# Two more slots in a weight ring of sixteen, a third gather from its own token numbers, and bias products ahead of gathered rows, in a hybrid decoder layer with 32 experts

## The reference

```python
logits = (xt @ w_router + b_router)          # 512 tokens, 32 experts
top_val, top_idx = lax.top_k(logits, 4)
gates = jax.nn.softmax(top_val, axis=-1)
# for each expert e and the rows xb that chose it:
hu = xb @ w1[e] + b1[e]                      # 1024 -> 2048
x_glu, x_lin = min(hu[:, :1024], 7), clip(hu[:, 1024:], -7, 7)
act = x_glu * sigmoid(1.702 * x_glu) * (x_lin + 1)
y = act @ w2[e] + b2[e]                      # 1024 -> 1024
# y times the gate is added to its token, then rmsnorm(x, g_final)
```

## Time and profile before

| | us |
|---|---|
| median of 3 runs | 1233.77 |
| lowest and highest run | 1233.51, 1235.34 |
| the profiled execution's own time | 1230.28 |
| its span | 1228.6 |
| TensorE products busy | 1152.6 (94%) |
| VectorE, ScalarE, GpSimd busy | 306.3, 191.4, 173.3 |
| DMA moved | 454.39 MB, mean 370 GB/s |

### The profile page before, as it was taken

How to read it: one execution, slowest core, us unless ns; L and a number is a source line. 1 busy time by engine, 2 the same in 40 slices (tenths; PEclk the granted TensorE clock), 3 DMA queues, 4 the chain that set the end, 5 groups by cost and what they waited for, 6 DMA issues and landing times. The chain is left out here.

```text
span 1228.6 us, 16404 instructions
## 1 busy us (share of the span) xinstructions
PE 1152.6 (94%) x7022; PEld 477.3 (39%) x7022; DVE 306.3 (25%) x484; ACT 191.4 (16%) x378; POOL 173.3 (14%) x250
## 2 busy tenths in 40 slices
PE   5999997899999999999999999999999999999980
PEld 4777786223333333333333323333333333333330
DVE  5678757321011010101101010110101011010118
ACT  5443522010110100001100000110000011000002
POOL 6000100521101111110111111111111111111000
PEclk9999998899999999999999999999999999999996
DMA  9500675699999999999999999999999999999996
GB/s 336 150 1 20 232 302 193 225 377 403 423 426 426 428 425 426 425 426 427 426 423 427 428 425 426 427 424 427 425 427 426 425 426 426 426 423 428 427 388 242
DMA packets 51147, 454.39 MB, mean 370 GB/s; under 512 B 13044, under 2 KB 13316, under 8 KB 26400
## 3 DMA queue, kind: packets, MB, share of 16 engines
q1 hardware_dynamic: 42864, 434.16, 85.2%
q0 software_dynamic: 7632, 17.05, 3.6%
q10 hardware_dynamic: 576, 2.10, 0.4%
HBM read 442.60 MB, written 15.12 MB: 373 GB/s over the span
## 5 line engine op out<-in xcount | busy, mean ns | idle before, releaser
L849 PE MATMUL ps<-ring_a,blockT 128*64 128x512 f32 x1472 | 325.3, 594 | 8.2 <-DMA ring_a<-in_w 8.1
L1310 DVE TENSOR_SCALAR xnT<-ps 128x768 f32<-128x768 f32 (+1 forms) x32 | 26.9, 841 | 814.7 <-PE ps L856 517.2
L849 PEld LDWEIGHTS ps<-ring_a,blockT 128*64 128x64 f32 x1472 | 101.8, 137 | 217.5 <-issue 195.0
L875 PE MATMUL ps<-ring_a,actT 128*64 128x512 f32 x736 | 165.3, 596 | 1.6 <-DMA ring_a<-in_w 1.6
L849 PE MATMUL ps<-ring_b,blockT 128*64 128x512 f32 x448 | 99.7, 595 | 6.3 <-DMA ring_b<-in_w 6.3
L1597 ACT ACTIVATE blockT<-ps 128x512 f32<-128x512 f32 x30 | 17.9, 597 | 553.0 <-PE ps L796 553.0
L1783 POOL DMA_INDIRECT scores<-h_rows,slots x30 | 31.7, 1056 | 505.7 <-PE ps L796 504.9
L856 PE MATMUL ps<-ring_a,blockT 128*32 128x512 f32 x768 | 91.5, 615 | 0.0
L875 PEld LDWEIGHTS ps<-ring_a,actT 128*64 128x64 f32 x736 | 49.9, 136 | 94.5 <-issue 89.6
L1799 POOL DMA_INDIRECT expert_rows<-normed,slots x32 | 32.6, 1019 | 269.9 <-ACT normed L1626 269.6
L875 PE MATMUL ps<-ring_b,actT 128*64 128x512 f32 x288 | 64.7, 596 | 0.0
(11 more groups left out here) (300 smaller groups left out, 1062.1 us busy)
## 6 DMA issues: line engine op xcount, KB each, us to landing
ring_a<-in_w SPq DMA_DIRECT2D x144, 2048.0 KB, 29.7
ring_b<-in_w SPq DMA_DIRECT2D x48, 2048.0 KB, 31.2
ring<-in_w_in SPq DMA_DIRECT2D x12, 768.0 KB, 18.3
ring<-expert_rows SPq DMA_DIRECT2D x16, 512.0 KB, 14.1
X<-in_x SPq DMA_DIRECT2D x8, 512.0 KB, 6.5
ring<-in_w_out SPq DMA_DIRECT2D x8, 512.0 KB, 4.6
h_rows<-normed ACTq DMA_DIRECT2D x4, 512.0 KB, 3.5
out<-ring SPq DMA_DIRECT2D x4, 512.0 KB, 2.6
```

Of the source, the lines that this page charges most:

```text
L849: ins = mm(ps[half * HALF:(half + 1) * HALF, b, :], x_of(k)[0], ring(r)[:, 0, at + half * 512:at + (half + 1) * 512], start=False, stop=(k ...
L875: ins = mm(ps[half * HALF:(half + 1) * HALF, bank, :], actT[:, s % 2 * W2_K + j, s // 2 * HALF:(s // 2 + 1) * HALF], ring(r)[:, 0, j * D + ...
L1310: v.tensor_scalar(width(glu_c, big), width(ps_glu, big), LIMIT, None, ALU.min).then_inc(glu_ready, 1)
```

## The change

The ring gets eighteen slots. The new two, `ring_c`, lie over `xnT`, and the activation buffers move from there to the memory behind `scores`, over `probsT`; `act_v` becomes the same buffer as `glu_c`. So the first pair of block 0's w2 goes to slots 16 and 17, waits only for the router's logits, and every later pair waits for a release that lies one pair further back. Since `act_v` is now `glu_c`, block 0's activations must be turned before block 1's are clamped: `turn_act_of(0)` moves into the middle of block 1's first product. The third block's token numbers are found as those of the first two (`PICKED = 3`): VectorE picks them ahead of `list_entries`, TensorE sums them in the middle of block 0's first product, and GpSimd gathers them behind its sixteen list writes. The bias products become a function of their own, `w1_bias`, which stands ahead of the wait for rows; for block 0 it stands ahead of the wait for the sort. The returned rows (`y_rows`) lie in slots 6 to 13.

```diff
-RING = 16
+RING = 18
+RING_B = 4
+ROWS_AT = 6
...
 STATIC = 2
+PICKED = 3
...
+        ring_c = sb_r("ring_c", [P, RING - PER - RING_B, SLOT], nc.sbuf_base - KT * SEQ * 4, F32)
...
+        work_at = nc.sbuf_base - HEADS * 2 * P * 4 - HEADS * P * 4
+        glu_c = sb_r("glu_c", [P, PART], work_at, F32)
+        lin_c = sb_r("lin_c", [P, PART], work_at + PART * 4, F32)
+        rowsT = sb_r("rowsT", [P, KT, MANY], work_at + 2 * PART * 4, F32)
+        blockT = sb_r("blockT", [P, 6, P], work_at + 2 * PART * 4, F32)
+        sig = sb_r("sig", [P, PART], work_at + 3 * PART * 4, F32)
+        act_v = glu_c
...
             load_first(12)
-            for k in range(0, W2_SLOTS, 2):
+            sp.wait_ge(logits_done, TB)
+            load_w2(0, 0, w2_slot(0, 0))
+            for k in range(2, W2_SLOTS, 2):
                 wait_free(w2_slot(0, k) + 1)
                 load_w2(0, k, w2_slot(0, k) % RING)
...
             mm(ps[0:E, 4, E:2 * E], ones_bf[:, 0:E], chosen_cum[:, TB, :], start=True, stop=True).then_inc(counts_done, 1)
+            pe.wait_ge(biases_ready, 2)
+            pe.wait_ge(cur_ready, 1)
+            w1_bias(BIG[0], 0)
             pe.wait_ge(sort_ready, 1)
...
+            def third_sums():
+
+                pe.wait_ge(pick_ready, 3 * TB)
+                for t in range(TB):
+                    for part in range(2):
+                        ins = mm(ps[:, 3, 0:1], pick[:, 0, t, :], tok_value[:, t, part:part + 1],
+                                 start=(t == 0 and part == 0), stop=(t == TB - 1 and part == 1))
+                ins.then_inc(tok_summed, 1)
+
             def first_product(i, parity):
 
-                pe.wait_ge(rows_ready, 2 * (i + 1))
-                pe.wait_ge(cur_ready, i + 1)
                 if i:
+                    pe.wait_ge(cur_ready, i + 1)
                     pe.wait_ge(glu_ready, i)
                     pe.wait_ge(lin_ready, i)
+                    w1_bias(BIG[i], parity)
+                pe.wait_ge(rows_ready, 2 * (i + 1))
                 w1_product(BIG[i], parity, lambda k: (w1_slot(i, k) % RING, *arrived[w1_slot(i, k)]),
-                           x_of_lines if i < STATIC else x_of_parts)
+                           x_of_lines if i < PICKED else x_of_parts,
+                           amid=(third_sums, lambda: turn_act_of(0))[i] if i < 2 else None)
...
-                if i == 1:
-                    turn_act_of(0)
...
+            def pick_third():
+
+                chosen_ranks, masked = (picked.rearrange("p t k e -> p (t k e)")[:, n * TB * E:(n + 1) * TB * E].rearrange("p (t e) -> p t e", t=TB) for n in range(2))
+                then(v.scalar_tensor_tensor(out=chosen_ranks, in0=chosen[:, :, :], scalar=-1024.0, in1=ranks[:, :, :], op0=ALU.mult, op1=ALU.add))
+                then(v.scalar_tensor_tensor(out=masked, in0=where[:, 0:E].unsqueeze(1).to_broadcast([P, TB, E]), scalar=float(PICKED - 1),
+                                            in1=chosen_ranks, op0=ALU.is_equal, op1=ALU.mult))
+                then(v.tensor_reduce(own_rank[:, :, 0], masked, AX_X, ALU.add))
+                for t in range(TB):
+                    v.tensor_scalar(pick[:, 0, t, :], iota_r[:, :], own_rank[:, t, 0:1], None, ALU.is_equal).then_inc(pick_ready, 1)
...
+            pick_third()
             list_entries()
+            third_tokens()
...
+            pool.wait_ge(tok_ready, 2)
+            pool.wait_ge(rows_turned, 2)
+            fetch(2)
             pool.wait_ge(list_written, 16 * (1 + TB * TOPK))
```

More of the change, by code:

```diff
@@ L53 @@
 MANY = HALF + QUARTER
+PART = MANY * KT
 HALVES, QUARTERS = range(2)
@@ L240, in layer_kernel, with y_rows @@
         gated_y = normed
-        glu_c, lin_c, sig, act_v = (xnT[:, 2 * n:2 * n + 2, :].rearrange("p k t -> p (k t)") for n in range(4))
         def ring(r, n=1):
-            return ring_a[:, r:r + n, :] if r < PER else ring_b[:, r - PER:r - PER + n, :]
-        y_rows = ring1[:, :].rearrange("p (k t n) -> p k t n", t=TB, k=TOPK)
+            if r < PER:
+                return ring_a[:, r:r + n, :]
+            if r < PER + RING_B:
+                return ring_b[:, r - PER:r - PER + n, :]
+            return ring_c[:, r - PER - RING_B:r - PER - RING_B + n, :]
+        def y_rows(k, t):
+            return ring(ROWS_AT + 2 * k, 2).rearrange("p j (h n) -> p (j h) n", h=TB // 2)[:, t, :]
         X_SUM, X_STD, X_R, A_STD, C_STD, H_SUM, H_STD, H_R, F_SUM, F_STD, F_R = range(0, 11 * TB, TB)
@@ L265, in layer_kernel @@
         bias_hi, bias_mid, bias_res = sem("bias_hi"), sem("bias_mid"), sem("bias_res")
-        slot_in = [sem(f"slot_in{r}") for r in range(RING)]
+        slot_in = {r: sem(f"slot_in{r}") for r in range(0, RING, 2)}
         dve_step, act_step, pool_step = sem("dve_step"), sem("act_step"), sem("pool_step")
@@ L514, in _ @@
                 sp.wait_ge(fin_ready, t + 1)
-                sp.dma_start(out[0, t * P:(t + 1) * P, :], y_rows[:, 0, t, :]).then_inc(out_written, 16)
+                sp.dma_start(out[0, t * P:(t + 1) * P, :], y_rows(0, t)).then_inc(out_written, 16)
             sp.wait_ge(out_written, 16 * TB)
@@ L746, in rank, with quarter_cols, w1_bias @@
                 ins.then_inc(rank_done, 1)
+            def quarter_cols(view, q):
+                cols = view.rearrange("p (g s n j) -> p g s n j", g=2, s=2, j=2 * W2_K)
+                return cols[:, :, q // 2, :, q % 2 * W2_K:(q % 2 + 1) * W2_K]
+            def w1_bias(big, parity):
+                for b, at in ((B_GLU, 0), (B_LIN, FF)):
+                    for half in range(2):
+                        mm(ps[half * HALF:(half + 1) * HALF, b, :], bias_sel[:, parity, half * HALF:(half + 1) * HALF],
+                           bias_split[:, at + half * 512:at + (half + 1) * 512], start=True, stop=False)
+                for q in range(4 if big else 0):
+                    mm(ps[q * QUARTER:(q + 1) * QUARTER, B_BOTH, :], bias_sel[:, parity, q * QUARTER:(q + 1) * QUARTER],
+                       quarter_cols(bias_split[:, 0:2 * FF], q),
+                       start=True, stop=False, tile_position=(0, q * QUARTER))
             attend(TB - 1)
@@ L826, in turn_act_of, with w1_product @@
                 turn(act_v, BIG[i], act_turned)
-            def quarter_cols(view, q):
-                cols = view.rearrange("p (g s n j) -> p g s n j", g=2, s=2, j=2 * W2_K)
-                return cols[:, :, q // 2, :, q % 2 * W2_K:(q % 2 + 1) * W2_K]
-            def w1_product(big, parity, slot, x_of):
-                for b, at in ((B_GLU, 0), (B_LIN, FF)):
-                    for half in range(2):
-                        mm(ps[half * HALF:(half + 1) * HALF, b, :], bias_sel[:, parity, half * HALF:(half + 1) * HALF],
-                           bias_split[:, at + half * 512:at + (half + 1) * 512], start=True, stop=False)
-                for q in range(4 if big else 0):
-                    mm(ps[q * QUARTER:(q + 1) * QUARTER, B_BOTH, :], bias_sel[:, parity, q * QUARTER:(q + 1) * QUARTER],
-                       quarter_cols(bias_split[:, 0:2 * FF], q),
-                       start=True, stop=False, tile_position=(0, q * QUARTER))
+            def w1_product(big, parity, slot, x_of, amid=None):
                 for k0 in range(0, KT, GROUP):
+                    if k0 and amid:
+                        amid()
                     for k in range(k0, k0 + GROUP):
@@ L1603, in turned_rows @@
                 act.wait_ge(rows_turned, i + 1)
-                if isinstance(i, int) and i < STATIC:
+                if isinstance(i, int) and i < PICKED:
                     for b in range(2):
@@ L1667, in _ @@
                 act.wait_ge(sum_ready, (TOPK - 1) * TB + t + 1)
-                a.activation(y_rows[:, 1, t, :], X[:, t, :], ACT.Square, accum_out=stat[:, F_SUM + t:F_SUM + t + 1]).then_inc(act_final, 1)
+                a.activation(y_rows(1, t), X[:, t, :], ACT.Square, accum_out=stat[:, F_SUM + t:F_SUM + t + 1]).then_inc(act_final, 1)
                 act.wait_ge(act_final, t + 1)
```

31 lines of the change are left out of this document (17 added, 14 removed).

## The result

The changed kernel takes **1227.19 us** (median of 9 runs, 1226.13 to 1230.94) beside 1233.51 us for the kernel before (9 runs, 1232.6 to 1236.36): ratio 0.9948, 95% interval 0.9936 to 0.996, so 6.3 us or 0.5% faster, outside the 0.2% that a measurement of this kernel leaves open. The forecast was 1227.7 us.

A forecast was written before the change was run, and what follows sets the result against it. The DMA engines were taken to set the end: the moment they never stop plus all bytes behind it at 426 GB/s. 4.92 + 0.65 + 0.6 less 0.1 gave 6.1 us, from 1233.77 to 1227.7 us; range 1224.8 to 1231.4 us.

The forecast's parts named there:

- The sum's last term: In the forecast sum: 131 KB more to move, taken as a loss of 0.1 us.
- Part 1: Ring of eighteen: block 0's early w2 pair fills the DMA engines' idle time from 226 to 235 us, gain 4.92 us.
- Parts 2 and 3: Block 0's bias products ahead of rows and eight sums amid its first product: TensorE releases slots 0.65 us earlier.
- the prediction's choice: Block 0's first product: the clock rises after unbroken work of whatever kind, so moving the biases wins only 0.90 us.
- its other case: Block 0's first product: the clock's rise moves along with the earlier start, so moving the biases wins 1.54 us.
- part 2: Block 0's bias products go ahead of the rows, into TensorE's wait for the sort: 0.90 us gained.
- Part 4: Third gather right behind the last list write, before the dip ends at 260 us: gain 0.6 us; lists 3 us later.
- Part 5: Block 0's activations turned amid block 1's first product: TensorE another 0.85 us ahead, which only adds to slack.
- (a): At the end: the pair is worth nothing because TensorE, not the supply, sets it; 1232.5 us, chance 0.10.
- (b): Between 257 and 300 us: part of the gain given back, 1.5 to 3 us lost; about 1230.3 us, chance 0.13.
- (c): More than forecast: clock rises with the work (0.64 us), TensorE's lead (0.85 us) reaches the loads; 1226.2 us, chance 0.14.
- (d): Small blocks: slower, GpSimd's gathers and scatters wait behind the weights of a longer queue; about 1242 us, chance 0.04.

The follow-up runs named there:

- third block by lists: Changed kernel with block 2's rows fetched by the lists again, without selection, sums or early third gather: 1229.23 us, ratio 0.9977 to the kernel before.
- more transposes: Changed kernel with the gathered rows of blocks 3 to 17 turned twice, 76 transposes more: 1237.54 us, ratio 0.9965 to the kernel before.
- ring of sixteen: Changed kernel with sixteen ring slots again and block 0's first w2 pair waiting for released slots: 1232.11 us, ratio 0.9987 to the kernel before.
- bias products behind: Changed kernel with block 0's bias products behind the wait for the rows again: 1230.04 us, ratio 0.9971 to the kernel before.
- groups of two slots: Changed kernel with blocks 0 and 1 worked in groups of two slots instead of four: 1229.4 us, ratio 0.9965 to the kernel before.
- before, third chip: The kernel before, unaltered, on the last group's chip, where TensorE stalls in block 0: 1240.44 us in one run.
- changed, third chip: The changed kernel, unaltered, on the last group's chip, where TensorE stalls in block 0: 1236.53 us, ratio 0.996 to the kernel before.
- depth without early load: Changed kernel with eighteen slots, but the load into the two new ones waits for the first release: 1235.77 us, ratio 0.9958 to the kernel before.
- early clamps: Changed kernel with VectorE clamping block 0's completed halves while TensorE runs the rest of the product: 1235.25 us, ratio 0.9953 to the kernel before.
- copy: The changed kernel, unaltered, as partner on the second group's chip: 1236.96 us, ratio 0.9973 to the kernel before.
- more products: Changed kernel with 26 unread bias-row products in TensorE's waits ahead of block 0: 1235.13 us, ratio 0.9957 to the kernel before.

## Why the prediction was right, step by step

One account holds for all fourteen profiles. In each, the stretch from 200 to 300 us has a mean rate (GB/s); times 100 us that is what was moved in it, and from 300 us on the rate is 426 GB/s (from 300 to 500 us 424 in the third block by lists, 425 with more transposes). If the DMA engines set the end, span plus moved bytes at 426 GB/s is a constant. Two of these rows, of the changed kernel and of the third block by lists:

```profile
200.00:300.00 100.00, 87.99 (x575) 34.99 (x574) 34.81 (x125) 13.31 (x29) 27.74 (x33) 0.91 0.91 340
```

```profile
200.00:300.00 100.00, 77.52 (x501) 32.32 (x501) 32.79 (x117) 13.04 (x28) 25.22 (x32) 0.83 0.81 294
```

| kernel | span, us | MB from 200 to 300 us | span + MB / 0.426 |
|---|---|---|---|
| before | 1228.6 | 32.3 | 1304.4 |
| changed | 1225.3 | 34.0 | 1305.1 |
| ring of sixteen | 1229.9 | 32.3 | 1305.7 |
| bias products behind | 1228.1 | 33.0 | 1305.6 |
| groups of two slots | 1225.0 | 34.3 | 1305.5 |
| third block by lists | 1237.0 | 29.4 | 1306.0 |
| before, third chip | 1238.8 | 28.4 | 1305.5 |
| changed, third chip | 1234.7 | 29.9 | 1304.9 |
| depth without early load | 1232.7 | 30.5 | 1304.3 |
| early clamps | 1231.0 | 31.2 | 1304.2 |

Spans that differ by 13.8 us have sums that differ by 1.8 us (the rates are whole GB/s, which leaves 0.1 us; the first 200 us are taken as equal, but their rates are 165 to 167 GB/s, which leaves up to 0.9 us). On the second chip the sums are 1304.5 (copy), 1304.4 (with 4.9 us taken off for its extra bytes), 1306.5 (more products) and 1307.3 us (more transposes); in these last two the first 200 us have the lowest rate, 165 GB/s. So the prediction's main sentence, the moment from which the engines never stop plus all bytes behind it, is what the runs show. The parts do not add up when each is taken back alone: 4.8, 2.8 and 2.0 us are lost, more than the whole 6.3 us, though each of these differences is uncertain by about 2 us. The sum's last term, 0.1 us for 131 KB more, is 0.3 us at 426 GB/s.

- **Part 1, 4.92 us**: the size held. Without slots and early load 4.8 us are lost. That it comes from the filled gap is not shown by itself: on a chip on which TensorE stalls, the two slots alone gave all of it. Its ground was narrower than the prediction said: "the pattern after 232.85 us is the old one with one pair more already done" needs a queue that does not run empty later. In the changed kernel it had only some 2 us in hand at 270 us (a landing in 10.2 us against 8.4 us for an empty queue).
- **Parts 2 and 3, 0.65 us**: the direction held (1.5 us earlier, 0.92 us kept with the sums' 0.28 us already off). What ends the slow time stays open: by the prediction's choice 0.64 us should come back in the first product, by its other case nothing; 0.30 us did against before (8.96 and 8.66 us), 0.59 us against the version with the bias products behind (8.37 us). The size is open too: taken back alone, part 2 costs 2.8 us, of which 1.0 us is the delay and 1.7 us a second fall of the clock.
- **Part 4, 0.6 us**: the wrong step, without effect on the sum. "The lists come 3 us later" was mis-sized: they came 14 us later (276.66 against 262.43 us). Of that the router and the selection are 4.1 us; the rest is the landing of writes and reads. The load that fills the gap explains little of it: from the last list write to the lists it is 14.8 us before and 24.9 us now, but 22.4 us with the gap back (ring of sixteen), 24.5 us without the third gather (third block by lists), and only 18.5 us in groups of two, where the engines are full from 226 us on. Before, the reads fell into the dip at 256 us; that this dip is the cause is likely but not tested. Had block 2 still waited for them, the change would have given 2 us less on the median and up to 12 us less in an execution. The gather's worth is that stall, not a filled dip. In the sum this did not show: with a ring of sixteen parts 2 to 4 give 1.3 us, near the forecast (1.2 us).
- **Part 5**: adds slack, as said; block 2's turn came without a wait. Block 3's rows, asked for at 276.66 us by the late lists, were turned at 299.88 us without a wait.
- **Rivals**: (a) fell by the extra transposes. (b) did not come in the changed kernel, but its place is real: groups of two slots and every kernel on the stalling chips lose bytes there. (c) is not needed. (d) did not come: a gather lands in 8.7 us both from 300 to 420 us and from 900 to 1150 us, with a queue of weights one pair longer.

## What to carry to other kernels

Where the DMA engines set the end, write down what they have moved by the moment from which they never stop: it gave the spans of ten profiles to within 2 us, and shows at once whether an early load is kept or handed back. Before filling the last idle stretches of the transfers, ask which small transfers had been living in them: the lists of this kernel came 14 us later, 10 us of them in their own writes and reads, and the next block is safe only because it no longer waits for them. Where the queue runs dry after a stall, a deeper ring alone is worth as much as with the earlier load (0.9958 and 0.996).

## What was not expected

- Small transfers beside full engines: four reads of 8 KB landed in 4.3 us with gaps around and in 8.6 us without, a gather of 96 lines took 15.3 us at 251 us (9.7 us in groups of two, beside engines just as full), while one of 128 half lines takes 8.7 us later with a longer queue.
- The granted clock stayed at 0.50 through 9.18 us of work in 10 us of 64-row products, and fell again in block 1 after a wait of 1.37 us in some executions and not in others (0.86 and 1.00 from 250 to 262 us).
- On two of the chips block 0's product takes 7.7 us (before) to 10.4 us (changed) longer, by stalls without a releaser. The kernel before is 7 to 8 us slower there, the changed kernel 9 to 10 us, so the same change is worth 6.3 us on one chip and 3.8 to 4.9 us on others.
